# Two mixture-of-experts stages: in-place dot product rows, and semaphores that count diagonals and products by fours

## Chip, cores and metric

The kernel runs on one core of one Trainium2 chip. The metric is the device time of one execution in microseconds, and each time below is the median of three runs.

## What is computed

Two transformer blocks follow each other on 256 tokens of width 1024, all in float32. Each ends in a "PEER" layer, the expert stage, and this is the part that the change touches. Cut to what matters:

```python
q = (xt @ w_pq).reshape(T, 8, 2, 128)              # T = 256 tokens, 8 heads
s = einsum('thpd,hpnd->thpn', q, subkeys)          # scores against 128 keys, twice per head
... top 16 of each, top 16 of their 256 sums ...   # 16 expert numbers per token and head
act = gelu(einsum('thkd,td->thk', peer_u[eb], xb)) * gb      # peer_u, peer_v: 16384 rows of 1024
out = einsum('thk,thkd->td', act, peer_v[eb])
```

For every token and each of its 8 x 16 = 128 experts, one row of `peer_u` is fetched for a dot product with the token, and one row of `peer_v` is fetched and added with the resulting weight. That is 256 x 128 x 2 rows of 4 KB per stage.

## The kernel before, in words

Tokens lie on the 128 partitions, in two tiles T. One "row" i of the stage (`ROWS` = 256, i = 0..255) is one expert slot of one tile: a gather by GpSimd (POOL) brings 128 table rows, one per partition, 512 KB. Rows 0 to 127 are tile 0 and rows 128 to 255 tile 1; sixteen rows in sequence are one head g of a tile. For each row i there is an up gather u(i) (`gather_u`, L2196) and a value gather v(i) (`gather_v`, L2211), 512 gathers per stage. Each engine has its own instruction order and only semaphores tie them together:

- **POOL** issues the gathers in a fixed order: u(0) to u(5), then value and up gathers in turn. Four value gathers are skipped around u(14) to u(21), so from there on the order is ..., v(j), u(j+10), v(j+1), u(j+11), ... An up row may be overwritten eight rows later, when its dot product is done (`u_used`). A value gather waits until the product that last used its slot is done (`pe_used`).
- **VectorE (DVE)** does the dot product of row i (L2038), writing the elementwise product to one of two junk buffers `uj` and the sum to `hidden`. It also does the top-k work of later heads, in parts between dot products, and `weigh(g)`: the weights of head g come right after the dot product of row 16(g+1).
- **ScalarE (ACT)** makes, for each row j, a 128x128 diagonal matrix of the 128 weights (L2162), in a ring of `DIAGS` = 12. It also copies query and score results of later heads out of PSUM (L2078, L2086).
- **TensorE (PE)** multiplies diagonal by value row (L2334) and accumulates in PSUM: two `mm` calls of 512 columns, which the trace shows as four MATMULs. This is called a product below. Before products 8, 20, 36 and 52 it computes a query (L2244, `QUERY_BEFORE`), and right after those products the query's scores (L2257).
- In the last head (rows 240 to 255) six of the rows are added by VectorE (L2061, `LAST_VEC`), so TensorE has 250 products per stage.

The value slots are a ring of `VRING` = 20, but eight of them hold query weights or up rows at first and are released one pair after each query. So the ring is short early in the stage (the code is `free`, `slots`):

```python
free = [(n + RING) % (VRING - RING) for n in range(VRING - RING)]     # 12 slots
slots = list(free)
for p in range(RAW):                                                  # RAW = 4
    slots += free + [VRING - RING + 2 * p, VRING - RING + 2 * p + 1]
```

Value row 12 takes the slot of row 0, row 20 that of row 8, row 34 that of row 20, row 50 that of row 36, row 51 that of row 37; rows 54 to 65 take slots used 14 rows before, and from about row 68 on it is the slot used 20 rows before.

Of the kernel before, what the change touches and what calls it, by code (L numbers as in the profile page):

```python
# [14 lines left out]
P = 128  # L15
S = 256
NT = S // P
# [29 lines left out]
U_AHEAD = 6  # L47
LEAD_GROWS = range(14, 22)
QUERY_BEFORE = {8: 6, 20: 7, 36: 8, 52: 9}
DIAGS = 12  # L50
LAST_IN_RING = 2
LAST_VEC = [2, 5, 7, 10, 13, 15]
SHIFTS = 3
# [1621 lines left out]
def stage_peer(K, rows, sk, nkeys, sk_dma, table_u, table_v, gelu, after, second, queries, out=None, unit=None):  # L1675
# [23 lines left out]
    with ExitStack() as ctx, nc.Block() as block:  # L1699
# [16 lines left out]
        xT = sb("xT", [P, KD, S])  # L1716
        ub = K.wring.rearrange("p a b -> p (a b)").rearrange("p (r d) -> p r d", d=D)
        first_row = 2 * K.query_slot
        uj = sb("uj", [P, D])[:, :], sb("uj", [P, D])[:, :]
        tss, tsd, tiv = (sb(n, [P, NT * after]) for n in ("tss", "tsd", "tiv"))  # L1720
        stored = sg("stored")
        diag = sb("diag", [P, DIAGS, P])
# [89 lines left out]
        def on_tensor(j):  # L1812
            return j if j < FIRST_LAST else FIRST_LAST + sum(1 for i in range(FIRST_LAST, j) if not on_vector(i))

        in_more = [j for j in range(ROWS) if slots[j] < VRING - RING]
        more_tensor, more_vector = ([j for j in in_more if on_vector(j) == which][-1] for which in (False, True))

# [8 lines left out]
        @block.sync  # L1826
        def _(sp):
            for p in queries[1]:
                if p in (2, 3):
                    sp.wait_ge(wlo.sem, PARTS * (second.units[p][0] + 1))  # L1830
                K.load_query(sp, queries[0], p, rows)
            K.reloads = second.units[-1][0] + 1
            K.load_gains(sp)
            sp.wait_ge(normed.sem, normed.at(NT))
            K.gains_used += 1
            K.load_gains(sp)
            if out is not None:
                for T in range(NT):
                    sp.wait_ge(normed.sem, normed.at(NT + T + 1))
                    sp.dma_start(out[T * P:(T + 1) * P, :], K.XN[:, T, :]).then_inc(stored.sem, stored.up(16))  # L1840
                sp.wait_ge(stored.sem, stored.n)
            else:
                sp.wait_ge(u_used.sem, u_used.at(ROWS))
                v_arrived(sp, ROWS - 3)
                K.load_limit = len(K.units)
                for n in range(RAW):
                    if n == RAW - 1:
                        sp.wait_ge(pe_used.sem, pe_used.at(ROWS - len(LAST_VEC)))
                        sp.wait_ge(vec_used.sem, vec_used.at(len(LAST_VEC)))
                    K.load_unit(sp)  # L1850

        @block.vector
        def _(v):
# [134 lines left out]
            def weigh(g):  # L1988

                v.wait_ge(g_exp.sem, g_exp.at(g + 1))  # L1990
                ve.reciprocal(ginv[:, g % 2:g % 2 + 1], gsum[:, g % 2:g % 2 + 1]).then_inc(g_inv.sem, 1)
                if g >= 2:
                    v.wait_ge(dia.sem, dia.at(TOPK * (g - 1)))
                v.wait_ge(g_inv.sem, g_inv.at(g + 1))
                v.wait_ge(act_r.sem, act_r.at(g + 1))
                ve.scalar_tensor_tensor(out=weight[:, g % 2, :], in0=active[:, g % 2, :], scalar=ginv[:, g % 2:g % 2 + 1],
                                        in1=gate[:, g % 2, :], op0=ALU.mult, op1=ALU.mult).then_inc(wts.sem, 1)

            def add_tokens(T):

                v.wait_ge(pe_used.sem, pe_used.at(on_tensor(PER_T * (T + 1))))
                ve.tensor_tensor(K.X[:, T, :], K.X[:, T, :], ps[:, 2 * T:2 * T + 2, :].rearrange("p b c -> p (b c)"),
                                 ALU.add).then_inc(out_r.sem, 1)

# [25 lines left out]
            for g in range(HEADS):  # L2030
                for s in range(TOPK):
                    i = g * TOPK + s
                    u_arrived(v, i)
                    if i >= 2:
                        v.wait_ge(u_used.sem, u_used.at(i - 1))
                    if i % PER_T == 0:
                        v.wait_ge(x_ps.sem, x_ps.at(g // PH + 1))
                    ve.scalar_tensor_tensor(out=uj[i % 2], in0=u_row(i), scalar=1.0, in1=tokens(g // PH),  # L2038
                                            op0=ALU.mult, op1=ALU.mult, accum_out=hidden[:, g % 2, s:s + 1]).then_inc(u_used.sem, 1)
                    if s == 0 and g:  # L2040
                        weigh(g - 1)
                    elif g == PH + 2 and s == TOPK - 2:
                        add_tokens(0)
                    for k in range(after):
                        if g == PH + 4 + 2 * k and s == 10:
                            scaled(v, 0, k)
                    for at, n in ((1, 1), (13, 2), (22, 3)):
                        if 0 <= i - at < TK_PARTS:
                            top_k(n, i - at)
                    if g >= 2 and g + 2 < HEADS and 1 <= s <= TK_PARTS:  # L2050
                        top_k(g + 2, s - 1)
# [19 lines left out]
        def _(act):  # L2071
# [73 lines left out]
            for g in range(HEADS):  # L2145
                act.wait_ge(u_used.sem, u_used.at(TOPK * (g + 1)))
                nc.scalar.activation(active[:, g % 2, :], hidden[:, g % 2, :], gelu).then_inc(act_r.sem, 1)
                act.wait_ge(wts.sem, wts.at(g + 1))
                for s in range(TOPK):
                    j = g * TOPK + s  # L2150
                    if on_vector(j):
                        continue
                    if j - 4 in QUERY_BEFORE:
                        query(QUERY_BEFORE[j - 4])
                        scored(QUERY_BEFORE[j - 4])
                        if QUERY_BEFORE[j - 4] == QSTEPS - 1:
                            act.wait_ge(q_out.sem, q_out.at(QSTEPS))
                            tokens_out(1)
                    n = on_tensor(j)
                    if n >= DIAGS:  # L2160
                        act.wait_ge(pe_used.sem, pe_used.at(n - DIAGS + 1))
                    nc.scalar.activation(diag[:, n % DIAGS, :], K.ident[:, :], ACT.Copy,  # L2162
                                         scale=weight[:, g % 2, s:s + 1]).then_inc(dia.sem, 1)
                for k in range(after):
                    if g == PH + 2 + 2 * k:
                        square(act, 0, k)
                if g + 1 < HEADS:
                    gate_exp(g + 1)
            if unit:
                act.wait_ge(pe_used.sem, pe_used.at(on_tensor(more_tensor) + 1))  # L2170
                act.wait_ge(vec_used.sem, vec_used.at(LAST_VEC.index(more_vector - FIRST_LAST) + 1))
                for half in range(2):
                    act.wait_ge(second.done.sem, second.base + len(second.units) + half + 1)
                    nc.scalar.activation(K.XNT[0][:, half * 4:half * 4 + 4, 0:P],
                                         ps[:, 2 * NT + half, :].rearrange("p (k t) -> p k t", k=4), ACT.Copy).then_inc(t_act.sem, t_act.up())
# [7 lines left out]
        def _(pool):  # L2183
# [15 lines left out]
            def gather_v(j):  # L2199

                n = v_slot(j)
                sig = v_in[n] if n < VRING else u_in[last_ring(n)]
                if n >= VRING:
                    pool.wait_ge(u_used.sem, u_used.at(ROWS))
                elif v_use(j):
                    pool.wait_ge(pe_used.sem, pe_used.at(max(m for m in range(j) if slots[m] == n) + 1))
                elif n >= VRING - RING:
                    home_free(pool, RAW + (n - VRING + RING) // 2)
                elif n < RING:
                    pool.wait_ge(u_used.sem, u_used.at(n + 1))  # L2210
                nc.gpsimd.indirect_dma_start(value_slot(n), None, table_v, bass.IndirectOffsetOnAxis(  # L2211
                    ap=idx[:, j // PER_T, j % PER_T:j % PER_T + 1], axis=0)).then_inc(sig.sem, 16)
# [14 lines left out]
        def _(pe):  # L2227
# [92 lines left out]
            for j in range(ROWS):  # L2320
# [4 lines left out]
                    query(QUERY_BEFORE[j])  # L2325
                if unit and j == FIRST_LAST - TOPK:
                    first_columns()
                pe.wait_ge(dia.sem, dia.at(n + 1))
                v_arrived(pe, j)
                if j == PER_T:  # L2330
                    pe.wait_ge(s_out.sem, s_out.at(QSTEPS))
# [1 line left out]
                for c in range(2):  # L2333
                    last = mm(ps[:, 2 * T + c, :], diag[:, n % DIAGS, :], value_slot(v_slot(j))[:, c * BANK:(c + 1) * BANK],  # L2334
                              start=j % PER_T == 0, stop=ends)
                last.then_inc(pe_used.sem, 1)
                if j in QUERY_BEFORE:
                    score(QUERY_BEFORE[j])
            if unit:
                first_product()  # L2340

        for sig, by in ((tk, TK_EARLY + TK_STEPS * HEADS), (picked, HEADS + 1), (u_used, ROWS), (pe_used, ROWS - len(LAST_VEC)),
                        (vec_used, len(LAST_VEC)), (dia, ROWS - len(LAST_VEC)), (out_r, NT), (x_ps, NT), (g_exp, HEADS), (g_inv, HEADS),
                        (act_r, HEADS), (wts, HEADS), (ready, HEADS),
                        (q_ps, QSTEPS), (q_out, QSTEPS), (s_ps, QSTEPS), (s_out, QSTEPS)):
            sig.up(by)
# [219 lines left out]
```

## Time and profile before

| | us |
|---|---|
| three unprofiled runs, median (lowest, highest) | 1973.23 (1970.73, 1973.85) |
| the profiled execution, first to last instruction | 2142.0 |
| PE busy | 1722.3 |
| DVE busy | 1254.5 |
| POOL busy | 1008.5 |
| ACT busy | 616.9 |

The page gives the profiled execution no other time than its span. It is 168.8 us (8.6%) longer than the unprofiled median, so durations of single instructions and gaps have to be read with care: some gaps of the trace don't exist without the profiler. Times of rows are microseconds from the span's start. In a row of the timeline the first number is the start, the second the duration, and the bracket at the end is the idle time of that engine before it and what ended that.

### The profile page before, as it was taken

The page shows a single profiled execution, that of the slowest core. Times are in us where ns is not written, and L with a number is a line of the kernel's source. Part 1 is how long each engine was busy: PE and PEld are TensorE (multiplying, and loading weights), DVE is VectorE, ACT ScalarE, POOL GpSimd, SP SyncE. Part 2 cuts the span into 40 slices and gives each one's busy share as a digit, 9 for nine tenths or more (in the row PEclk, how much of TensorE's full clock was granted, in tenths as well). Part 3 has the DMA queues.
Part 4 walks back from the last instruction along what each step waited for, and adds up shares of the span by engine and source line. Part 5 has one row for each costly group of instructions (what it writes and reads, how often), then busy time and mean ns, then how long its engine had stood idle before and what let it go on. Part 6 is the DMA issues. An engine that isn't in the chain of part 4 may idle for free. (4 is left out here: it accounts for less than half of the span.)

```text
span 2142.0 us, 22067 instructions
## 1 busy us (share of the span) xinstructions
PE 1722.3 (80%) x7643; PEld 1082.0 (51%) x7643; DVE 1254.5 (59%) x2789; ACT 616.9 (29%) x1151; POOL 1008.5 (47%) x1095
## 2 busy tenths in 40 slices
PE   8999999978787686768668999877777867677768
PEld 7998898844443232323224999754442322222323
DVE  6544665885565665566453456685555566476553
ACT  4472644412121111222213455312212111212212
POOL 3021000366666666667672000265666666666663
PEclk9998999989998787878778999898997878788878
DMA  7521553999999999999997756598999999999996
GB/s 253 165 82 60 172 188 116 307 365 341 347 371 373 351 367 383 352 366 368 361 391 241 232 161 197 187 338 332 342 367 375 361 364 370 365 372 370 359 376 240
DMA packets 243719, 644.22 MB, mean 301 GB/s; under 512 B 19541, under 2 KB 105354, under 8 KB 243610
## 3 DMA queue, kind: packets, MB, share of 16 engines
q0 software_dynamic: 147456, 536.94, 66.3%
q1 hardware_dynamic: 96154, 105.88, 15.4%
q8 instruction: 62, 1.02, 0.2%
q14 instruction: 47, 0.39, 0.0%
HBM read 641.69 MB, written 1.05 MB: 300 GB/s over the span
## 5 line engine op out<-in xcount | busy, mean ns | idle before, releaser
L2038 DVE SCALAR_TENSOR_TENSOR ex_uj<-wring,ps 128x1024 f32<-128x1024 f32 x496 | 601.8, 1219 | 409.7 <-DMA wring<-in_peer_u,ex_idx 363.7
L2334 PE MATMUL ps<-ex_v,ex_diag 128*128 128x512 f32 x1328 | 664.6, 647 | 168.4 <-issue 162.6
L2196 POOL DMA_INDIRECT wring<-in_peer_u,ex_idx x496 | 468.6, 945 | 176.1 <-issue 141.4
L2334 PEld LDWEIGHTS ps<-ex_v,ex_diag 128*128 128x128 f32 x1328 | 270.6, 206 | 546.2 <-issue 535.0
L2334 PE MATMUL ps<-value_rows,ex_diag 128*128 128x512 f32 x664 | 360.0, 677 | 135.4 <-issue 134.0
L2211 POOL DMA_INDIRECT ex_v<-in_peer_v,ex_idx x336 | 318.1, 947 | 242.3 <-remote 110.8
L2162 ACT ACTIVATE ex_diag<-ident,ex_weight 128x128 f32<-128x128 f32 x500 | 171.0, 393 | 720.0 <-remote 390.1
L2334 PEld LDWEIGHTS ps<-value_rows,ex_diag 128*128 128x128 f32 x664 | 141.7, 215 | 351.0 <-issue 345.4
L208 DVE TENSOR_TENSOR w_lo<-wring,w_hi 128x1024 fp32r<-128x1024 f32 (+1 forms) x160 | 187.3, 1211 | 108.4 <-ACT w_hi L199 106.1
L2196 POOL DMA_INDIRECT ex_v<-in_peer_u,ex_idx x16 | 16.4, 1023 | 464.1 <-PE ps L283 459.9
L2211 POOL DMA_INDIRECT value_rows<-in_peer_v,ex_idx x172 | 164.2, 955 | 96.3 <-remote 47.2
L199 ACT ACTIVATE w_hi<-wring 128x1024 fp32r<-128x1024 f32 (+1 forms) x160 | 158.2, 1039 | 80.8 <-PE ps L575 35.3
L575 PE MATMUL ps<-XNT_high,w_hi 128*128 128x256 f32 x328 | 94.1, 287 | 0.5 <-DVE w_lo L208 0.3
L575 PE MATMUL ps<-XNT_low,w_hi 128*128 128x256 f32 x328 | 93.8, 286 | 0.0
L575 PE MATMUL ps<-XNT_high,w_lo 128*128 128x256 f32 x328 | 93.7, 286 | 0.0
L245 PE MATMUL ps<-XNT_high,w_hi 128*128 128x256 f32 x288 | 86.3, 300 | 1.0 <-PEq L510 1.0
L245 PE MATMUL ps<-XNT_low,w_hi 128*128 128x256 f32 x288 | 82.4, 286 | 0.0
L245 PE MATMUL ps<-XNT_high,w_lo 128*128 128x256 f32 x288 | 82.3, 286 | 0.0
L2078 ACT ACTIVATE ex_query<-ps 128x512 f32<-128x512 f32 (+1 forms) x20 | 10.2, 511 | 244.1 <-remote 216.3
L2244 PE MATMUL ps<-ex_xT,wring 128*128 128x128 f32 (+1 forms) x384 | 61.1, 320 | 9.5 <-DVE ex_xT L1985 7.6
L2244 PE MATMUL ps<-ex_xT,value_rows 128*128 128x256 f32 x256 | 58.2, 380 | 11.4 <-issue 11.4
L575 PEld LDWEIGHTS ps<-XNT_high,w_hi 128*128 128x128 f32 x328 | 64.0, 195 | 1.0 <-issue 1.0
(470 smaller groups left out, 2465.0 us busy)
## 6 DMA issues: line engine op xcount, KB each, us to landing
wring<-in_w_in SPq DMA_DIRECT2D x42, 1024.0 KB, 5.4
wring<-in_w_ckv SPq DMA_DIRECT2D x8, 1024.0 KB, 5.3
wring<-in_peer_u,ex_idx POOLq DMA_INDIRECT x496
ex_v<-in_peer_v,ex_idx POOLq DMA_INDIRECT x336
wring<-in_w_mix_out SPq DMA_DIRECT2D x4, 1024.0 KB, 6.6
wring<-in_w_cq SPq DMA_DIRECT2D x4, 1024.0 KB, 5.1
wring<-in_w_co SPq DMA_DIRECT2D x4, 1024.0 KB, 5.2
value_rows<-in_w_pq SPq DMA_DIRECT2D x4, 1024.0 KB, 10.3
```

What stands on the lines that cost most here:

```text
L199: self.nc.scalar.activation(self.part(self.w_hi, m, b), self.raw_part(m, b), ACT.Copy).then_inc(self.named("weights_high").sem, 1)
L208: self.nc.vector.tensor_tensor(self.part(self.w_lo, m, b), self.raw_part(m, b), self.part(self.w_hi, m, b).bitcast(F32), ALU.subtract).the ...
L245: last = mm(ps[:, 6 + u % 2, c * S:(c + 1) * S], w[:, i, c * P:(c + 1) * P], x[:, i, :], start=i == 0 and p == 0, stop=i == KD - 1 and p == 2)
L575: last = nc.tensor.matmul(ps[:, bank_of(j), c * S:(c + 1) * S], w[:, i, off + c * P:off + c * P + P], x[:, i, :], start=start, stop=stop, ...
L2038: ve.scalar_tensor_tensor(out=uj[i % 2], in0=u_row(i), scalar=1.0, in1=tokens(g // PH), op0=ALU.mult, op1=ALU.mult, accum_out=hidden[:, g ...
L2078: nc.scalar.activation(qT[:, k % 2, :, t0 * P:t1 * P], ps[:, query_bank(k), :].rearrange("p (c t) -> p c t", c=2)[:, :, t0 * P:t1 * P], AC ...
L2162: nc.scalar.activation(diag[:, n % DIAGS, :], K.ident[:, :], ACT.Copy, scale=weight[:, g % 2, s:s + 1]).then_inc(dia.sem, 1)
L2196: nc.gpsimd.indirect_dma_start(u_row(i), None, table_u, bass.IndirectOffsetOnAxis(ap=idx[:, g // PH, i % PER_T:i % PER_T + 1], axis=0)).th ...
L2211: nc.gpsimd.indirect_dma_start(value_slot(n), None, table_v, bass.IndirectOffsetOnAxis(ap=idx[:, j // PER_T, j % PER_T:j % PER_T + 1], axi ...
L2244: last = mm(ps[:, query_bank(k), c * S + t0 * P:c * S + t1 * P], w[:, i, c * P:(c + 1) * P], xT[:, i, t0 * P:t1 * P], start=c == 0 and i = ...
L2334: last = mm(ps[:, 2 * T + c, :], diag[:, n % DIAGS, :], value_slot(v_slot(j))[:, c * BANK:(c + 1) * BANK], start=j % PER_T == 0, stop=ends)
```

## The change

Two edits, both in the expert stages.

1. The dot product's elementwise output goes over the up row that it reads (`out=u_row(i)`) and no longer to `uj`, and the wait for the dot product two rows earlier, which protected the junk buffer, is gone.
2. `dia` (diagonals made) and `pe_used` (products done) are increased once for each group of four consecutive TensorE rows (`DIAG_GROUP` = 4; the last group has two), not once for each. Everyone who waits for one of them waits for the group: TensorE before the first product of a group for four diagonals, ScalarE before the first diagonal of a group for the group that used its ring places, POOL before a value gather for the whole group in which the slot's last product lies.

```diff
-DIAGS = 12
+DIAGS, DIAG_GROUP = 12, 4
...
-        uj = sb("uj", [P, D])[:, :], sb("uj", [P, D])[:, :]
...
+        def group(j):
+            return on_tensor(j) // DIAG_GROUP
+
+        def groups(j):
+            return -(-on_tensor(j) // DIAG_GROUP)
+
+        TENSOR_ROWS = ROWS - len(LAST_VEC)
+
+        def ends_group(n):
+            return n % DIAG_GROUP == DIAG_GROUP - 1 or n == TENSOR_ROWS - 1
...
-                    v.wait_ge(dia.sem, dia.at(TOPK * (g - 1)))
+                    v.wait_ge(dia.sem, dia.at(groups(TOPK * (g - 1))))
...
                     u_arrived(v, i)
-                    if i >= 2:
-                        v.wait_ge(u_used.sem, u_used.at(i - 1))
...
-                    ve.scalar_tensor_tensor(out=uj[i % 2], in0=u_row(i), scalar=1.0, in1=tokens(g // PH),
+                    ve.scalar_tensor_tensor(out=u_row(i), in0=u_row(i), scalar=1.0, in1=tokens(g // PH),
...
-                    if n >= DIAGS:
-                        act.wait_ge(pe_used.sem, pe_used.at(n - DIAGS + 1))
-                    nc.scalar.activation(diag[:, n % DIAGS, :], K.ident[:, :], ACT.Copy,
-                                         scale=weight[:, g % 2, s:s + 1]).then_inc(dia.sem, 1)
+                    if n >= DIAGS and n % DIAG_GROUP == 0:
+                        act.wait_ge(pe_used.sem, pe_used.at((n - DIAGS) // DIAG_GROUP + 1))
+                    made = nc.scalar.activation(diag[:, n % DIAGS, :], K.ident[:, :], ACT.Copy,
+                                                scale=weight[:, g % 2, s:s + 1])
+                    if ends_group(n):
+                        made.then_inc(dia.sem, 1)
...
-                    pool.wait_ge(pe_used.sem, pe_used.at(max(m for m in range(j) if slots[m] == n) + 1))
+                    pool.wait_ge(pe_used.sem, pe_used.at(group(max(m for m in range(j) if slots[m] == n)) + 1))
...
-                pe.wait_ge(dia.sem, dia.at(n + 1))
+                if n % DIAG_GROUP == 0:
+                    pe.wait_ge(dia.sem, dia.at(group(j) + 1))
                 v_arrived(pe, j)
...
-                last.then_inc(pe_used.sem, 1)
+                if ends_group(n):
+                    last.then_inc(pe_used.sem, 1)
```

No instruction that computes or moves data is added, removed or moved in an engine's order; waits and increments are all that changes, beside the output address.

## Rows read from the trace of the kernel before

**Rows 1.** The page: its span, and the gathers' queue (packets, MB, share).

```profile
span 2142.0 us, 22067 instructions
q0 software_dynamic: 147456, 536.94, 66.3%
```

**Rows 2.** Timeline, POOL: first gathers of the stages, waiting value gathers, u(48).

```profile
404.93 1.17 POOL L2196 DMA_INDIRECT ex_v<-in_peer_u,ex_idx  x1 [236.95 <-PE ps L283]
...
455.72 0.94 POOL L2211 DMA_INDIRECT ex_v<-in_peer_v,ex_idx  x1 [2.48 <-issue]
...
474.87 0.94 POOL L2196 DMA_INDIRECT wring<-in_peer_u,ex_idx  x1 [0.30 <-issue]
479.26 0.94 POOL L2211 DMA_INDIRECT ex_v<-in_peer_v,ex_idx  x1 [3.44 <-remote]
...
482.76 0.94 POOL L2211 DMA_INDIRECT ex_v<-in_peer_v,ex_idx  x1 [1.22 <-PE ps L2334]
...
514.70 0.94 POOL L2196 DMA_INDIRECT wring<-in_peer_u,ex_idx  x1 [0.30 <-issue]
521.85 0.94 POOL L2211 DMA_INDIRECT ex_v<-in_peer_v,ex_idx  x1 [6.22 <-PE ps L2334]
...
533.61 0.94 POOL L2196 DMA_INDIRECT wring<-in_peer_u,ex_idx  x1 [0.30 <-issue]
...
1368.80 0.94 POOL L2196 DMA_INDIRECT ex_v<-in_peer_u,ex_idx  x1 [222.93 <-PE ps L283]
```

**Rows 3.** Windows of 5 us: length, busy by engine, clock, DMA share, GB/s.

```profile
480.00:485.00 5.00, 5.00 (x18) 2.61 (x18) 3.63 (x11) 4.15 (x9) 3.12 (x4) 1.00 0.76 233
485.00:490.00 5.00, 5.00 (x13) 2.18 (x12) 1.23 (x3) 0.69 (x2) 3.76 (x4) 1.00 0.87 269
515.00:520.00 5.00, 2.22 (x3) 1.07 (x4) 1.11 (x6) 0.17 (x1) 0.64 (x1) 0.55 1.00 400
520.00:525.00 5.00, 5.00 (x16) 2.77 (x16) 4.97 (x14) 2.48 (x8) 1.97 (x3) 0.76 0.31 93
525.00:530.00 5.00, 5.00 (x13) 2.17 (x12) 4.93 (x12) 3.95 (x8) 3.78 (x5) 1.00 0.88 301
535.00:540.00 5.00, 5.00 (x13) 2.18 (x12) 2.43 (x4) 0.21 (x1) 3.78 (x5) 1.00 1.02 415
```

**Rows 4.** Lines by tile: the stages' last TensorE products.

```profile
L2334 PE MATMUL ps<-wring,ex_diag x8: 592/592/593, 1163.9 to 2134.0; 128*128 128x512 f32 x8
```

**Rows 5.** Timeline, ACT: the first diagonals of stage one, and a late one.

```profile
451.21 3.61 ACT L2162 ACTIVATE ex_diag<-ident,ex_weight 128x128 f32<-128x128 f32 x12 [2.13 <-issue]
...
704.53 0.40 ACT L2162 ACTIVATE ex_diag<-ident,ex_weight 128x128 f32<-128x128 f32 x1 [10.10 <-issue]
```

**Rows 6.** Timeline, PE and its weight loads: products, queries, scores.

```profile
451.66 16.89 PE L2334 MATMUL ps<-ex_v,ex_diag 128*128 128x512 f32 x32 [11.49 <-issue]
468.39 7.07 PE L2244 MATMUL ps<-ex_xT,value_rows 128*128 128x256 f32 x32
...
479.61 1.16 PE L2257 MATMUL ps<-sk,ex_query 128*128 128x128 f32 x8 [2.43 <-ACT ex_query L2078]
480.61 9.61 PE L2334 MATMUL ps<-ex_v,ex_diag 128*128 128x512 f32 x22
...
514.59 0.38 PE L2244 MATMUL ps<-ex_xT,value_rows 128*128 128x256 f32 x1 [2.41 <-issue]
517.39 1.01 PE L2334 MATMUL ps<-ex_v,ex_diag 128*128 128x512 f32 x1 [2.42 <-issue]
...
542.16 7.13 PE L2334 MATMUL ps<-ex_v,ex_diag 128*128 128x512 f32 x16 [0.37 <-issue]
...
832.73 0.19 PEld L2334 LDWEIGHTS ps<-value_rows,ex_diag 128*128 128x128 f32 x1 [0.24 <-issue]
```

**Rows 7.** Groups by line: the dot products, and VectorE's last-head additions.

```profile
L2038 DVE SCALAR_TENSOR_TENSOR ex_uj<-wring,ps 128x1024 f32<-128x1024 f32 x496 | 601.8, 1219 | 409.7 <-DMA wring<-in_peer_u,ex_idx 363.7 <-issue 41.7 <-remote 1.8
L2061 DVE SCALAR_TENSOR_TENSOR X<-value_rows,ex_weight,X x3: 1273/1275/1283, 1140.0 to 1158.6; 128x1024 f32<-128x1024 f32 x3
```

More of the change, by code:

```diff
@@ L1847, in _ @@
                     if n == RAW - 1:
-                        sp.wait_ge(pe_used.sem, pe_used.at(ROWS - len(LAST_VEC)))
+                        sp.wait_ge(pe_used.sem, pe_used.at(groups(ROWS)))
                         sp.wait_ge(vec_used.sem, vec_used.at(len(LAST_VEC)))
@@ L1999, in add_tokens @@
             def add_tokens(T):
-                v.wait_ge(pe_used.sem, pe_used.at(on_tensor(PER_T * (T + 1))))
+                v.wait_ge(pe_used.sem, pe_used.at(groups(PER_T * (T + 1))))
                 ve.tensor_tensor(K.X[:, T, :], K.X[:, T, :], ps[:, 2 * T:2 * T + 2, :].rearrange("p b c -> p (b c)"),
@@ L2169, in _ @@
             if unit:
-                act.wait_ge(pe_used.sem, pe_used.at(on_tensor(more_tensor) + 1))
+                act.wait_ge(pe_used.sem, pe_used.at(group(more_tensor) + 1))
                 act.wait_ge(vec_used.sem, vec_used.at(LAST_VEC.index(more_vector - FIRST_LAST) + 1))
@@ L2340, in _ @@
                 first_product()
-        for sig, by in ((tk, TK_EARLY + TK_STEPS * HEADS), (picked, HEADS + 1), (u_used, ROWS), (pe_used, ROWS - len(LAST_VEC)),
-                        (vec_used, len(LAST_VEC)), (dia, ROWS - len(LAST_VEC)), (out_r, NT), (x_ps, NT), (g_exp, HEADS), (g_inv, HEADS),
+        for sig, by in ((tk, TK_EARLY + TK_STEPS * HEADS), (picked, HEADS + 1), (u_used, ROWS), (pe_used, groups(ROWS)),
+                        (vec_used, len(LAST_VEC)), (dia, groups(ROWS)), (out_r, NT), (x_ps, NT), (g_exp, HEADS), (g_inv, HEADS),
                         (act_r, HEADS), (wts, HEADS), (ready, HEADS),
```

## Prediction, made before the changed kernel ran

> **What bounds the kernel now.** I read the page's head first, then windows of the expert stages, then POOL's timeline, in which the row numbers come from counting the gathers along the code's order from the first. The gathers are 536.94 MB of the traffic [rows 1] and run from 404.93 to just after 1163.9 us and from 1368.80 to just after 2134.0 [rows 2, 4]: 761 and 767 us, together 1528 with what follows the last product. All other work is 2142 - 1528 = 614 us, and the change doesn't touch it. Without the profiler the median is 1973.2, so the two stages take about (1973.2 - 614) / 2 = 680 us each. That is the number to explain. One gather is 536.94 MB / 1024 = 0.524 MB. The full rate of a window is 415 GB/s [rows 3], which is 1.263 us a gather and 647 us for 512. POOL issues a gather every 0.94 + 0.30 = 1.24 us when nothing holds it [rows 2], 637 us for 512. The two paces are within 2% of each other, and each fills all but some 35 us of the 680; first arrivals, waits early in the stage and the last products take the rest. So an expert stage is a stream of gathers with no reserve, and whatever holds POOL's queue is paid unless transfers are piled up behind it.
>
> Are they? Look at u at 514.70 followed by v(34) at 521.85 [rows 2]: 7.15 us between issues in place of 1.24, so POOL missed 5.9. The windows there carried 400, 93 and 301 GB/s, against 415 later [rows 3]: that is 0.2 + 3.9 + 1.4 = 5.5 us of lost transfer. At v(20) and v(21) POOL missed 3.1 + 1.0 = 4.1, and the windows at 233 and 269 GB/s lost 2.2 + 1.8 = 4.0. **A wait of POOL is lost nearly one for one**; the pile covers about half a microsecond.
>
> The 169 us by which the profiled execution is longer are stretches in which all engines crawl together: a diagonal after 10.1 us of idleness, matmuls 2.4 us apart [rows 5, 6]. The arithmetic above (680 against 647) leaves no room for them without the profiler, so I take them out wherever they stand in the steps below.
>
> **The change part by part.**
>
> *In-place dot product and its removed wait.* The output row costs nothing or little: 1219 ns now with its output elsewhere; VectorE's other operation of this kind writes over its own input from SBUF at 1275 [rows 7]. The bounds are 0 and +56 ns, 29 us of VectorE over both stages; it lies in the 363.7 us in which VectorE waits for gathers anyway. Without that cover, in the first 30 rows of a stage where VectorE has top-k work, it would be 30 x 0.056 = 1.7 us a stage. The nearest row to the new form is its own old form (one input in PSUM), so I take 0. The removed wait was for a dot product two rows back on the same in-order engine, satisfied whenever it is reached: 0.
>
> *Fewer increments and waits, TensorE and ScalarE.* Per stage 187 waits for `dia` and 187 increments of `pe_used` go. Weight loads of products in one burst are 0.19 + 0.24 = 0.43 us apart, four to a product, 1.72 [rows 6]; loads of a burst stand at this pitch inside a product and from one product to the next, so the wait and the increment cost nothing that a pitch read to 0.01 us shows. I take 0; the other end is 0.02 us a product, 10 us for the 500 of both stages, if TensorE's chain set the end. The Trainium skill speaks otherwise ("TensorE: Matmul & The Clock Gate", section "The cost: per-tile semaphore tail"): increments on completion serialize at some 26 ns each. By that rule 374 fewer would give about 10 us, 1963. No run here shows it, and the row of the weight loads has no such gap.
>
> *Four diagonals before the first product.* Diagonals are 3.61 / 12 = 0.30 apart [rows 5]. Where TensorE waits for a head's first diagonal it now starts 3 x 0.30 = 0.9 us later.
>
> *Slots freed by fours.* This is the term that counts, and it is a new wait. POOL's queue holds up gathers behind a value gather: of both kinds, the up rows for the next head included.
> 1. **v(12)** needs product 0, and was issued at 455.72 after 2.5 us of idleness. It will need product 3. The 32 MATMULs from 451.66 are products 0 to 7, ending at 468.55; 4 x 1.72 before that, 461.67, product 3 ends. With 0.9 for the diagonals and 0.27 to the issue: 462.8, 7.1 later.
> 2. **v(20)** needs product 8, issued at 479.26; it will need product 11. Products 9, 10, 11 run from 480.61, ending at 485.8; +0.9 + 0.27: 487.0, 7.7 later. This doesn't add to the first, since head 0's products don't depend on gathers still to come; the later v(12) is absorbed in it. v(21), which waited for product 9 and was issued at 482.76, follows 2.49 behind at 489.5: from here POOL is **6.7** late.
> 3. **v(34)** needs product 20, which will be 23; its chain starts at u(32), which is now late with POOL, so a delay here adds. Take the same loop one head later for durations: u(48) at 533.61 to product 32 at 542.16 is 8.55; four products 7.13; a query 7.07; the fifth product 1.72; sum 24.5 [rows 2, 6]. POOL gets from u(32) to v(34) in 1.24 + 11 x 2.49 = 28.6. So without the slow stretch (POOL waited 6.22 there only because the query and product 20 crawled) it doesn't wait now, with 3.9 to spare. After: + 0.9, + scores 1.16, + 3 x 1.72 = 7.2, so 31.7 + 0.27 against 28.6: **3.3**.
> 4. **v(50)**: needs product 36, then 39, with query 8 between: the same loop from u(48), another **3.3**.
> 5. Later: v(54) needs product 43, 4 x 1.72 = 6.9 after 39, and comes 10 us later: free. From row 68 the slot is 20 rows old. v(16g+20) comes 33.6 us after u(16g+16), and its group is done 8.55 + 0.9 + 7.1 = 16.6 after it; 17 us to spare. The diagonal ring: diagonal n waits for product n - 9 in place of n - 12, still 8 products (13.8 us) ahead of 1.2 us of work.
>
> Sum per stage: 6.7 + 3.3 + 3.3 = 13.3 us of POOL, of which piled-up transfers cover 0.5 a wait and somewhat more at the first, 2 in all: 11.3 lost. They aren't won back, since transfers at 1.263 are slower than POOL at 1.24. Stage two has the same code with the same first phase. Two stages: +22.6 us. Against the profiled execution that is 2142 + 23 = 2165, there perhaps more, since with slow stretches v(34) and v(50) have no spare; against the median 1973.2 + 22 = **1995 us**, 1.1% slower.
>
> **The rivals.**
> - *Faster: instructions that only wait do cost.* Gone are 254 waits of VectorE and 187 of TensorE a stage, by the code, 882 of the 22067 instructions [rows 1]. If a product has the 0.02 us of its own that the pitch can hide, 10 us come back (500 x 0.02) while the new waits are covered: 1963. For it: the crawl exists, its cause isn't in the rows, and part of the 33 us a stage over the 647 could be of its kind. Against: the even pitch of 0.43, and a TensorE with idle time between heads. The rule of "TensorE: Matmul & The Clock Gate" above would come out at this time too. It decides if the waits of 1, 3 and 4 together lose under 5 us a stage. Chance 0.14.
> - *No change: POOL's new waits are covered.* More transfers are piled up without the profiler than in the windows, or the loops 3 and 4 keep their spare of 3.9 plus a few, and the first wait is won back before row 60. Then 1973, within 4 us. Against: 5.5 of 5.9 us lost at v(34). Chance 0.17.
> - *Only the first wait remains*, 6.7 - 1 a stage, the loops being shorter than I took them: 1985. Part of "slower", 0.20.
> - *Forecast*, all three waits, 1989 to 2002: 0.40.
> - *More than that*: nothing covered (13.3), the last head's products 0.9 later at the end of the stage where value rows and products finish together, the in-place cost of 1.7: 15.9 x 2 = 32, 2005 or above. Chance 0.09.
>
> **How the numbers follow.** The likeliest case gives 1995. Its own range is 1989 to 2002. For 8 in 10 the range has to take in the covered case and leave most of the faster one out: 1968 to 2005. A measurement of this kernel tells 0.2% (4 us) from no change. Faster 0.14, same 0.17, slower 0.69.
>
> **What would show it.** In the changed kernel's timeline v(12) is issued some 7 us later after its up gather than now, and v(13) to v(15) follow without any wait; v(20), v(34) and v(50) wait for PE, longer than v(12)'s present 2.5 us; the 5 us windows behind them fall under 300 GB/s; v(21), v(35), v(51) don't wait. Dot products remain at 1219 ns and products at 1.72. Behind row 68 no value gather waits for PE outside of a slow stretch. I'm wrong if POOL's time from its first gather to v(60) doesn't grow by some 10 us, if the windows stay full through the new waits, or if the products' pitch falls below 1.72, which would make the first rival right.

## The result, and the profile after

The changed kernel is 1.3% slower: 1994.89 us (median of 4, 1992.99 to 1998.98) against 1971.98 for the kernel before (median of 4, 1966.92 to 1973.85). The ratio is 1.0131, 95% interval 1.011 to 1.0151. The forecast was 1995.0. The two medians are 22.9 us apart, 11.5 a stage, against 11.3 in the sum. The ratio isn't exactly the quotient of the medians (that is 1.0116 here) and says 25.8 us, 12.9 a stage. A repetition below, with 22 runs of the kernel before and again four of the changed one, puts the ratio at 1.0139, some 14 us a stage, so the sum was somewhat low. Four single executions among the runs below took 3258 to 7518 us and are left out of every ratio.

First the page of the changed kernel: head, clock and rate over 40 slices of the span, and the dot product's group.

```profile
span 1997.3 us, 21187 instructions
PEclk9989799998899888888889999988999877888779
GB/s 251 178 85 44 118 202 190 162 338 336 369 377 409 409 410 409 409 409 409 409 409 372 253 179 121 225 331 349 367 379 409 409 409 409 409 409 409 410 409 307
L2046 DVE SCALAR_TENSOR_TENSOR wring<-wring,ps 128x1024 f32<-128x1024 f32 x496 | 605.4, 1221 | 429.5 <-DMA wring<-in_peer_u,ex_idx 426.2
```

880 instructions are gone from the program (22067 in [rows 1]), the dot product takes 1221 ns where it took 1219 [rows 7], and once a stage is well under way the gathers stream at a flat 409 GB/s. Within a stage the rate is below that in its first three or four slices (336, 369, 377; then 331, 349, 367, 379) and in its last. The execution timed with this profile took 1998.98 us and its span is 1997.3: nothing separates profiled and unprofiled time here.

Next the timeline of POOL in the changed kernel, the same places as in [rows 2]. In order: u(0), u(21), v(12), v(13), v(20), v(21), u(32), v(34), v(35), v(50), v(51).

```profile
411.34 1.17 POOL L2206 DMA_INDIRECT ex_v<-in_peer_u,ex_idx  x1 [242.39 <-PE ps L283]
...
454.73 0.93 POOL L2206 DMA_INDIRECT wring<-in_peer_u,ex_idx  x1 [0.30 <-issue]
465.33 0.94 POOL L2221 DMA_INDIRECT ex_v<-in_peer_v,ex_idx  x1 [9.67 <-PE ps L2345]
...
467.81 0.94 POOL L2221 DMA_INDIRECT ex_v<-in_peer_v,ex_idx  x1 [0.30 <-issue]
...
486.87 0.93 POOL L2221 DMA_INDIRECT ex_v<-in_peer_v,ex_idx  x1 [1.71 <-PE ps L2345]
...
489.34 0.94 POOL L2221 DMA_INDIRECT ex_v<-in_peer_v,ex_idx  x1 [0.30 <-issue]
...
493.07 0.94 POOL L2206 DMA_INDIRECT wring<-in_peer_u,ex_idx  x1 [0.31 <-issue]
...
526.96 0.93 POOL L2221 DMA_INDIRECT ex_v<-in_peer_v,ex_idx  x1 [4.86 <-PE ps L2345]
...
529.44 0.94 POOL L2221 DMA_INDIRECT ex_v<-in_peer_v,ex_idx  x1 [0.30 <-issue]
...
572.01 0.94 POOL L2221 DMA_INDIRECT ex_v<-in_peer_v,ex_idx  x1 [5.04 <-PE ps L2345]
...
574.49 0.94 POOL L2221 DMA_INDIRECT ex_v<-in_peer_v,ex_idx  x1 [0.30 <-issue]
```

The gap in front of v(12) is 9.67 us, where it was 2.48; v(34) and v(50) wait 4.86 and 5.04. The gathers with a lower number in the same group (v(13), v(35), v(51)) wait for nothing, because one increment frees all four slots. This is what the forecast asked the reader to look for, with one exception: it had v(20) wait longer than 2.5 us, and the wait is 1.71.

What the gaps do to the transfers is in the windows of 5 us (columns as in [rows 3]; the last is GB/s):

```profile
460.00:465.00 5.00, 5.00 (x13) 2.19 (x12) 4.93 (x13) 0.00 (x0) 0.00 (x0) 0.99 0.09 34
465.00:470.00 5.00, 5.00 (x13) 2.18 (x12) 0.07 (x2) 0.00 (x0) 3.74 (x4) 1.00 0.56 174
470.00:475.00 5.00, 5.00 (x20) 3.61 (x19) 2.14 (x8) 0.00 (x0) 3.75 (x4) 1.00 0.91 297
485.00:490.00 5.00, 5.00 (x13) 2.23 (x12) 3.85 (x12) 1.36 (x2) 2.68 (x4) 1.00 1.03 407
525.00:530.00 5.00, 5.00 (x13) 2.13 (x12) 2.03 (x4) 2.59 (x5) 2.43 (x3) 1.00 0.42 129
530.00:535.00 5.00, 5.00 (x13) 2.24 (x12) 1.23 (x2) 0.00 (x0) 3.78 (x5) 1.00 0.94 316
535.00:540.00 5.00, 5.00 (x13) 2.09 (x11) 1.70 (x3) 0.00 (x0) 3.78 (x5) 1.00 0.98 367
```

Against 409, the first three lose 4.6 + 2.9 + 1.4 = 8.8 us for a gap of 9.67, and the last three 3.4 + 1.1 + 0.5 = 5.1 for 4.86. Only v(20) loses nothing (407): its gap of 1.71 is short enough for what is piled up. Here the forecast's sign, a window under 300 behind each wait, didn't come either.

### The profile page after: what moved, and what is told of

Read it like the earlier page. It is cut to its first block and busy times, and to the rows that moved or that the text cites. A ratio compares the mean times of both kernels' runs of the same rounds, so it can differ in the third digit from the quotient of the medians.

```text
span 1997.3 us, 21187 instructions
## 1 busy us (share of the span) xinstructions
PE 1639.4 (82%) x7643; PEld 1072.9 (54%) x7643; DVE 1261.6 (63%) x2789; ACT 600.5 (30%) x1151; POOL 1003.8 (50%) x1095
## 5 line engine op out<-in xcount | busy, mean ns | idle before, releaser
L2046 DVE SCALAR_TENSOR_TENSOR wring<-wring,ps 128x1024 f32<-128x1024 f32 x496 | 605.4, 1221 | 429.5 <-DMA wring<-in_peer_u,ex_idx 426.2
L2345 PE MATMUL ps<-ex_v,ex_diag 128*128 128x512 f32 x1328 | 631.5, 634 | 212.1 <-ACT ex_diag L2170 210.2
L2345 PE MATMUL ps<-value_rows,ex_diag 128*128 128x512 f32 x664 | 312.0, 626 | 95.3 <-ACT ex_diag L2170 94.1
L2345 PEld LDWEIGHTS ps<-value_rows,ex_diag 128*128 128x128 f32 x664 | 132.1, 201 | 268.8 <-issue 163.0
L2170 ACT ACTIVATE ex_diag<-ident,ex_weight 128x128 f32<-128x128 f32 x500 | 152.9, 388 | 239.2 <-PE ps L2345 159.1
L2155 ACT ACTIVATE ex_active<-ex_hidden 128x16 f32<-128x16 f32 x32 | 6.9, 215 | 609.8 <-DVE wring L2046 609.8
L575 PEld LDWEIGHTS ps<-XNT_high,w_lo 128*128 128x128 f32 x328 | 63.7, 194 | 0.0
## 6 DMA issues: line engine op xcount, KB each, us to landing
value_rows<-in_w_pq SPq DMA_DIRECT2D x4, 1024.0 KB, 10.1
```

The costliest lines, as they stand in the source:

```text
L575: last = nc.tensor.matmul(ps[:, bank_of(j), c * S:(c + 1) * S], w[:, i, off + c * P:off + c * P + P], x[:, i, :], start=start, stop=stop, ...
L2046: ve.scalar_tensor_tensor(out=u_row(i), in0=u_row(i), scalar=1.0, in1=tokens(g // PH), op0=ALU.mult, op1=ALU.mult, accum_out=hidden[:, g % ...
L2170: made = nc.scalar.activation(diag[:, n % DIAGS, :], K.ident[:, :], ACT.Copy, scale=weight[:, g % 2, s:s + 1])
```

## The experiments

Each was timed in five rounds against the kernel before on the same chip; every ratio is to that. The first four ran on one chip, on which every kernel, the one before too, takes nearly 9% longer (2140.32 against 1968.21), so a ratio, and no time, is carried from one chip to another. The next four rows of the table ran on a second chip and the last four on a third, both of the usual speed. All but the repetition of the change are built on one variant of it, in which the size of a group is a function of the row number, for each semaphore by itself:

```diff
-DIAGS, DIAG_GROUP = 12, 4
+DIAGS = 12
+DIA_SIZE, PE_SIZE = (lambda n: 4), (lambda n: 4)
```

| | time | before | ratio | 95% |
|---|---|---|---|---|
| in place only | 2138.54 | 2140.32 | 0.9993 | 0.9975 to 1.0011 |
| groups only | 2159.49 | 2140.32 | 1.0083 | 1.006 to 1.0106 |
| diagonals by four | 2139.75 | 2140.32 | 0.9997 | 0.9981 to 1.0014 |
| products by four | 2159.62 | 2140.32 | 1.0082 | 1.0059 to 1.0106 |
| the whole change | 1994.26 | 1968.21 | 1.0139 | 1.0124 to 1.0154 |
| both by two | 1970.74 | 1968.21 | 1.0014 | 1.0002 to 1.0027 |
| two more slots | 1961.64 | 1968.21 | 0.9968 | 0.9956 to 0.998 |
| two more slots, by four | 1969.24 | 1968.21 | 1.0004 | 0.9991 to 1.0017 |
| fours from row 68 | 1967.33 | 1968.41 | 0.9999 | 0.999 to 1.0009 |
| fours until row 68 | 1994.56 | 1968.41 | 1.014 | 1.0124 to 1.0157 |
| in place only, again | 1966.13 | 1968.41 | 0.9992 | 0.9981 to 1.0002 |
| products by four, again | 1987.84 | 1968.41 | 1.0105 | 1.0091 to 1.012 |

### The parts, each alone

**In place only.** The dot product over its up row, its wait gone, both semaphores counted by ones.

```diff
+DIA_SIZE, PE_SIZE = (lambda n: 1), (lambda n: 1)
```

> The dot product over its own up row and without its wait; diagonals and products counted one by one, as before. Slot theory (the loss is value gathers held up because slots come free by fours): no such wait here, so the time of before, 1972, within 4 us. Rival (instructions that only wait cost time): 508 of the 882 are gone, so some 6 us come back, 1966. Rival (the in-place write slows VectorE): 1976 or more, with the dot product's mean above 1221 ns. The profiled execution of before was 2142 and that of the changed kernel 1997.3: if the crawling stretches come with VectorE's extra wait instructions, this one is profiled at about 1975; if they come with the semaphore traffic of ScalarE and TensorE, at about 2140.

**Groups only.** Both by four, dot products into `uj` with their wait, as before.

```diff
-                    ve.scalar_tensor_tensor(out=u_row(i), in0=u_row(i), ...
+                    if i >= 2:
+                        v.wait_ge(u_used.sem, u_used.at(i - 1))
+                    ve.scalar_tensor_tensor(out=uj[i % 2], in0=u_row(i), ...
```

> Junk buffers and their wait kept; diagonals and products counted by fours. Slot theory: all of the loss, 1995 within 4 us. Rival (the in-place write is part of the loss): clearly under 1995. Profiled: the opposite of the run with the in-place row alone, about 2140 if VectorE's waits make the crawl, about 2000 if the one-by-one counting does.

**Diagonals by four**, products by ones.

```diff
+DIA_SIZE, PE_SIZE = (lambda n: 4), (lambda n: 1)
```

> In-place row; diagonals counted by fours, products one by one. Slot theory: slots come free as before, only the first product of a head starts 0.9 us later (three more diagonals); that moves v(12) and v(20) by 0.9 and is within the spare of the later ones: 1 us a stage, 1974. Rival (TensorE's later start is the loss, through heads that follow each other without a gap): 16 heads by 0.9 a stage, 29 us, 2001.

**Products by four**, diagonals by ones.

```diff
+DIA_SIZE, PE_SIZE = (lambda n: 1), (lambda n: 4)
```

> In-place row; products counted by fours, diagonals one by one. Slot theory: the loss without the 0.9 us: v(12) 6.2 late, POOL 5.8 late after v(21), then 2.5 at v(34) and 2.5 at v(50), less 2 covered: 8.8 a stage, 1990. Rival (diagonals by fours are the loss): 1972.

In place only is 0.9993 and, on a chip of the usual speed, 0.9992: no change that can be told. Groups only is 1.0083 and products by four 1.0082: on this chip counting the products by four is the whole loss. Diagonals by four alone are 0.9997.

The traces of the faster chips have no stretches in which all engines crawl, so two of the four were repeated on one, each as it is above:

> The in-place row alone a second time, since its first measurement was on a chip where all kernels took 2140 us. If this chip is like that of the changed kernel (before near 1970): ratio 1.000, as there (0.9993). Rival (without the long stretches the removed waits of VectorE show): 0.997.

> Products by fours, diagonals one by one, a second time for the same reason. Where before takes 1970: slot theory without the 0.9 us, 17.6 us, ratio 1.009; what is missing to the changed kernel's 1.013 is the diagonals' part, v(12) and the loops of v(34) and v(50) each 0.9 later. Rival (the diagonals' 0.9 us is free, as their own run said): 1.013.

**The change itself** once more, with more runs of the kernel before.

> The changed kernel itself once more, beside the others of this group. In the last group of runs the kernel before took 2140 us, 8.5% more than in the first measurement, and all its neighbours with it, so a time is read by its ratio to the kernel before on the same chip. Slot theory: a ratio of 1.009 to 1.013, as products by fours alone gave 1.008 there. If the longer time comes with the chip, the kernel before lies near 1972 or near 2140 and nowhere between.

It is 1.0139, and products by four are 1.0105, on another chip of the same speed. Fours until row 68, below, has diagonals by four too and ran on the same chip as products by four: 1.014. So on these chips the diagonals add some 0.0035 (6.7 us) once products are by four. On the slower chip they added nothing, alone (0.9997) or with the products (1.0083 against 1.0082), and on a faster chip they weren't timed alone. That the 0.9 us go into waits with room when they come alone, and lie in front of waits without room in the change, is argued from the table below and not shown by a run.

### Where in the stage

**Fours from row 68, ones before**, and **fours until row 68, ones after**: the first removes only instructions behind the early waits, the second replaces the early waits only.

```diff
+DIA_SIZE, PE_SIZE = (lambda n: 1 if n < 68 else 4), (lambda n: 1 if n < 68 else 4)
```

> In-place row; rows 0 to 67 counted one by one, from row 68 on by fours (both semaphores). Slot theory: from row 68 the slot is 20 rows old and nothing waits, so nothing is lost: ratio 1.000, although 91 of the 125 or so groups of a whole stage, and with them most of the removed waits, are there. Rival (the later start of each head by 0.9 us, or any cost of fours in the long middle part, is the loss): 12 of 16 heads, 1.010. Rival (fewer semaphore operations are worth something): 0.996.

```diff
+DIA_SIZE, PE_SIZE = (lambda n: 4 if n < 68 else 1), (lambda n: 4 if n < 68 else 1)
```

> The complement: in-place row, rows 0 to 67 counted by fours, all later ones one by one. Slot theory: the whole loss of the changed kernel, ratio 1.012 to 1.014. Rival (loss spread over the stage): a quarter of it, 1.003.

The split is complete: 0.9999 and 1.014. The whole loss is in the first 68 of 256 rows, and the fewer waits and increments of the other 182 products of a stage (272 instructions fewer by the pages of this kernel and of in place only, 21289 against 21561) give nothing that can be told.

POOL's list of waits shows the same (total, times, longest). The four rows, in this order, are of the change, of in place only (again), of both by two and of two more slots:

```profile
POOL ex_v L2221 <- PE ps L2345: 43.0, 22, 9.7
```
```profile
POOL ex_v L2225 <- PE ps L2349: 25.4, 58, 3.1
```
```profile
POOL ex_v L2225 <- PE ps L2349: 22.1, 21, 5.6
```
```profile
POOL ex_v L2227 <- PE ps L2351: 16.2, 53, 0.3
```

With many entries of 0.3 in such a row (the 0.3 that every gather has in front of it), the longest says more than the total.

The table is POOL's position at six places: issue of the value gather minus issue of u(0), mean of both stages, from the timelines. In stage one of the change v(12) is 465.33 - 411.34 = 53.99. For in place only (again), which stands for the kernel before here, u(0), v(12), v(34) and v(50) of stage one are:

```profile
404.25 1.17 POOL L2210 DMA_INDIRECT ex_v<-in_peer_u,ex_idx  x1 [235.44 <-PE ps L285]
...
451.66 0.93 POOL L2225 DMA_INDIRECT ex_v<-in_peer_v,ex_idx  x1 [3.06 <-PE ps L2349]
...
507.90 0.93 POOL L2225 DMA_INDIRECT ex_v<-in_peer_v,ex_idx  x1 [0.30 <-issue]
...
547.66 1.18 POOL L2225 DMA_INDIRECT ex_v<-in_peer_v,ex_idx  x1 [0.30 <-issue]
```

| us after u(0) | v(12) | v(20) | v(34) | v(50) | v(60) | v(255) |
|---|---|---|---|---|---|---|
| in place only | 46.9 | 68.2 | 103.3 | 143.1 | 168.2 | 657.1 |
| the change (profile after), later by | 6.9 | 7.1 | 12.2 | 17.4 | 17.2 | 14.2 |
| fours until 68, later by | 6.6 | 6.8 | 11.9 | 17.1 | 16.9 | 14.3 |
| products by four, later by | 6.7 | 6.9 | 9.8 | 13.9 | 13.7 | 10.9 |
| both by two, later by | 3.0 | 3.1 | 3.9 | 5.0 | 4.9 | 3.0 |
| fours from 68, later by | 0.8 | 0.1 | 0.3 | 0.4 | 0.2 | 0.4 |

Twice the last column is the loss: the change is 1.0139 - 0.9992 = 0.0147 of 1968 us slower than in place only, 28.9 us, or 14.5 a stage against 14.2; products by four 22.2 us, 11.1 a stage against 10.9. For both by two it fits less well: 4.3 us, 2.2 a stage against 3.0, from one trace and an interval of about 0.001 on either side.

### How the loss depends on the slack

**Both by two.**

```diff
+DIA_SIZE, PE_SIZE = (lambda n: 2), (lambda n: 2)
```

> As the changed kernel, with groups of two in place of four. Slot theory: v(12) waits for product 1 and v(20) for product 9, which puts POOL 2.8 us late after v(21); at v(34) and v(50) 24.5 + 0.3 + 1.16 + 1.72 + 0.27 = 28.0 stays under 28.6, so neither waits. 2.3 us a stage, 4.6 in all: ratio 1.0023. Rival (a loss that grows evenly with the group, a third of 23): 7.7 us, ratio 1.004. Rival (the number of semaphore operations counts): faster than before, 0.998.

A third of the group's extra products costs a fifth (3.0 of 14.2): v(20) is 3.1 late, but v(34) and v(50) together add only 1.9. The expectation that these two wouldn't wait at all was wrong: v(34) waits 1.9 us in stage one, v(50) 1.5 in both stages.

**Two more slots.** The junk buffers' 8 KB a partition hold two more value rows. In place, both by ones, and the slots of the last rows put in an order that fits 22:

```diff
-RING, VRING = 8, 20
+RING, VRING = 8, 22
...
+DIA_SIZE, PE_SIZE = (lambda n: 1), (lambda n: 1)
...
-            slots.append(min(range(VRING), key=lambda n: max(j for j, m in enumerate(slots) if m == n)))
+            left = len(slots) - (ROWS - LAST_IN_RING - VRING)
+            among = range(VRING) if left < 0 else range(VRING - RING) if left < VRING - RING else range(VRING - RING, VRING)
+            slots.append(min(among, key=lambda n: max(j for j, m in enumerate(slots) if m == n)))
```

> In-place row, everything counted one by one, and the 8 KB a partition that the junk buffers freed used for two more value slots (22, of them 14 from the start; the last 22 rows take their slots in an order that leaves the stage's end as it is). Row 14, not 12, is the first to take a used slot, row 22 follows row 8. Slot theory: the waits of before at v(12), v(20) and v(21) (2.2 + 3.1 + 0.9 us) go too, POOL is 6 us earlier after row 22 and 5 of them reach the end: 10 us faster in all, ratio 0.995. Rival (POOL's waits early in the stage are covered by piled-up transfers, and the loss of the change has another source): 1.000.

**Two more slots, both by four.** The same with groups of four.

> As the changed kernel, counted by fours, with the two more value slots. Slot theory: v(14) waits for product 3 until 462.8, v(22) for product 11 until 487.0, where the kernel before issued v(22) at 485.25: 1.8 us later; v(36), which now takes the slot of row 20, comes 5 us later in POOL's order than v(34) and doesn't wait. 1.8 us a stage, ratio 1.002. Rival (the loss has to do with fours as such, not with which row waits): 1.011.

With both by one it is 0.9968: 6.3 us faster than the kernel before, where 10 were expected, and the only version here that beats it. Its longest wait for a slot is 0.3 (above). The new order of the last slots wasn't tried without the two slots. With fours and two more slots the ratio is 1.0004: the same coarse count that costs 27 us on a ring of 20 leaves nothing to be told from the kernel before on one of 22, though it still costs 7 us against the same ring by ones; where those lie, no trace here shows. The same run limits another reading of products by four: that edit also makes ScalarE wait for whole groups before it makes diagonals. This wait is the same on the ring of 22, so at most those 7 us can be its doing, and the rest is the wait for slots.

## Why the prediction was right, and where it wasn't

**The stream of gathers with no reserve: right.** So was the step that a wait of POOL is lost nearly one for one: 8.8 of 9.67 and 5.1 of 4.86 us above. Over the 150 us in which all the new waits lie the rate is 360 GB/s in the change (first row) and 402 in the in-place kernel (second), and after it both hold 409:

```profile
451.00:601.00 150.00, 122.43 (x327) 63.71 (x328) 98.02 (x270) 30.46 (x81) 97.37 (x104) 0.89 0.93 360
```
```profile
444.00:594.00 150.00, 135.72 (x385) 73.06 (x386) 109.34 (x299) 36.05 (x93) 110.15 (x117) 0.94 1.02 402
```

150 x (402 - 360) / 409 = 15.4 us. The cover of 2 us was too small, though: of the 17.2 us by which POOL is late at v(60), 3.0 are back at v(255). The full rate is 409 and not the 415 of one window [rows 3]: 1.282 us a gather. So POOL at 1.24 has more room to catch up with the transfers than I took. (512 x 1.24 is 635 us and not 637, which changes nothing else, and the sum itself gives 1973.2 + 22.6 = 1995.8.)

**In place, and instructions that only wait, at nothing: right.** 0.9992 and 0.9993 with 506 instructions fewer (21561 against 22067 in [rows 1]); 0.9999 with 272 waits and as many increments of each semaphore less. The time alone doesn't prove that an increment is free, because behind row 68 the gathers set the pace (409 GB/s in both kernels). TensorE's own pace does: eight products follow each other in the same time in the in-place kernel (first), with an increment at each, and in the change, with one at every fourth.

```profile
617.45 13.90 PE L2349 MATMUL ps<-value_rows,ex_diag 128*128 128x512 f32 x32
```
```profile
639.62 13.90 PE L2345 MATMUL ps<-value_rows,ex_diag 128*128 128x512 f32 x32
```

The Trainium skill ("TensorE: Matmul & The Clock Gate", section "The cost: per-tile semaphore tail") states some 26 ns for each increment, measured on small matmuls that run side by side in the array. By this figure the six increments fewer would have made the second row an estimated 0.16 us shorter, and the trace doesn't agree. The first rival falls with the times and with this row.

The removed waits of VectorE cost nothing that shows either. The Trainium skill ("VectorE: DVE Perf Modes", section "The DRAIN you can't avoid") states that a semaphore after each operation costs nothing extra. The times of in place only agree (0.9992 and 0.9993), but VectorE also idles for gathers for 426.2 us in the profile after, so a small cost wouldn't show in them.

**Step 1 and 2, v(12) and v(20): right in size.** 7.1 was forecast and 6.9 measured for the first, 6.7 and 7.1 for POOL after both, and the second swallows the first as it should (6.9, then 7.1, not 14).

**Steps 3 and 4, v(34) and v(50): the mechanism right, the size wrong.** I took 3.3 each and 5.2 were measured (7.07 to 12.24 and on to 17.39, the table's means with one digit more). The term at fault is the "four products 7.13" of the loop. That row [rows 6] has 0.37 us of idle TensorE in front of it and runs at the full clock. In the changed kernel TensorE has waited longer when a head begins. First the change from product 16 on, then the in-place kernel:

```profile
501.90 10.12 PE L2345 MATMUL ps<-ex_v,ex_diag 128*128 128x512 f32 x16 [8.44 <-ACT ex_diag L2170]
511.86 0.38 PE L2254 MATMUL ps<-ex_xT,value_rows 128*128 128x256 f32 x1
```
```profile
488.70 8.83 PE L2349 MATMUL ps<-ex_v,ex_diag 128*128 128x512 f32 x16 [3.23 <-ACT ex_diag L2174]
497.37 7.07 PE L2258 MATMUL ps<-ex_xT,value_rows 128*128 128x256 f32 x32
```

The four products take 9.96 us from start to the next query's start (511.86 - 501.90) after 8.44 of idleness, and 8.67 after 3.23. The granted clock says why, again the change first (two windows) and then the in-place kernel:

```profile
500.00:505.00 5.00, 3.10 (x4) 1.51 (x5) 3.54 (x13) 2.45 (x8) 3.78 (x5) 0.50 1.03 410
505.00:510.00 5.00, 5.00 (x9) 1.96 (x8) 4.12 (x16) 0.00 (x0) 3.78 (x5) 0.71 1.02 408
```
```profile
488.00:493.00 5.00, 4.29 (x7) 1.83 (x8) 3.61 (x13) 2.45 (x8) 3.78 (x5) 0.69 1.03 409
493.00:498.00 5.00, 5.00 (x14) 2.48 (x13) 4.13 (x13) 0.00 (x0) 3.78 (x5) 0.97 1.03 411
```

0.50 is 1.2 of the 2.4 GHz. The Trainium skill ("TensorE: Matmul & The Clock Gate", section "Part 1: The HAM clock gate") states that the array gets half its clock after an idle time. The trace agrees, with these windows. So the loop feeds on itself: POOL late, weights late, TensorE idle for longer, its first products of the head at the lower clock, the group's last product later, v(34) later.

The length of the idle time alone doesn't fix the duration, though. In stage two of the in-place kernel the same four products take 7.13 us after 1.97 of idleness (the clock is 1.00 there); those of the next head take 9.95 after 6.00, more than the 9.45 after 7.20 in the change:

```profile
1364.24 7.13 PE L2349 MATMUL ps<-ex_v,ex_diag 128*128 128x512 f32 x16 [1.97 <-ACT ex_diag L2174]
1405.78 9.95 PE L2349 MATMUL ps<-ex_v,ex_diag 128*128 128x512 f32 x16 [6.00 <-ACT ex_diag L2174]
```
```profile
547.62 9.45 PE L2345 MATMUL ps<-ex_v,ex_diag 128*128 128x512 f32 x16 [7.20 <-ACT ex_diag L2170]
```

What the two long ones share is the granted clock at their start, 0.50 (the in-place kernel first, then the change):

```profile
1405.00:1410.00 5.00, 4.22 (x5) 1.85 (x6) 3.61 (x13) 2.45 (x8) 3.78 (x5) 0.50 1.03 410
547.00:552.00 5.00, 4.38 (x5) 1.85 (x6) 4.29 (x16) 1.74 (x6) 3.78 (x5) 0.50 1.03 407
```

From u(32) to v(34) it measures 526.96 - 493.07 = 33.9 against my 32.0 (the 24.5 with its additions and the 0.27 to the issue). Of the 1.9 too few, the four products are 2.8 too few; from u(32) to product 16 I had 0.6 too many (8.55 + 0.9 against 501.90 - 493.07 = 8.83), and for the query, the scores and the last four products 0.3 too many. The spare of 3.9 which I gave v(34) holds only where the four products run at the full clock: between the end of the product that it needs and its issue, less the 0.27, there are 4.4 us in stage two of the in-place kernel and 1.5 in stage one (product 20 ends at 506.16, as the trace models it, and v(34) is issued at 507.90). v(50) has 0.2 and 0.0.

The two misses have opposite signs but don't cancel. POOL was 4 us later at v(60) than the sum (17.2 against 13.3), and 1 us more was won back (3.0 against 2), so a stage loses 14.2 and not 11.3. That the forecast of 1995.0 meets the first median of 1994.89 to a tenth is luck: the kernel before measured 1971.98 in those four runs and 1968.2 beside the repetition, where the changed one measured 1994.3.

**Later rows free: right**, by fours from row 68 (0.9999).

**Four diagonals at 0.9: right at the place, wrong as a term of the sum.** From the first diagonal to the first product it is 455.76 - 454.43 = 1.33 us in the change and 447.60 - 447.15 = 0.45 in the in-place kernel. In the table, the change against products by four, that makes 0.2 at v(12) and v(20), where the two stages of one kernel differ by more (53.3 and 53.8 in products by four), then 2.3 at v(34) and 1.0 at v(50), and 3.3 a stage at the end. At v(34) the clock comes on top of the 0.9: products by four has the four products in 500.12 - 491.12 = 9.00 us, the change in 9.96.

**The step that was wrong outright** is the one in which the 169 us of the profile of before were called the profiler's ("leaves no room for them without the profiler, so I take them out"). They belong to the chip, as far as the runs can tell (on which chip the profile of before was taken is not on record). On the chip of the first four experiments 23 timed runs of the kernel before have a median of 2140.32, and the in-place kernel has a span of 2135.9 there and of 1961.5 on another, the same kernel under the same profiler. The crawl that I saw in the rows of before is in TensorE's list of waits (total, times, longest) of its trace. The trace of in place only on the slower chip has such a row too (274.8, 183, 11.6), and those of the change and of in place only on the faster chips have none, so neither the profiler nor the edits make it:

```profile
PE ps L2334 <- issue: 296.6, 208, 11.5
```

The derivation of 680 us a stage survived only because it started from a median of the faster chips (u(0) to the end of the last product is 672 us in the in-place kernel there). On the slower chip the change loses less than on the other (1.0083 against 1.0139, the former with `uj` kept), not more, as the prediction had supposed for stages with slow stretches.

Of the rivals, "no change" fell with the windows at 34 and 129 GB/s, and "only the first wait" with v(34) and v(50). "More than that" had the size of what POOL does but not the time: 2005 would have needed 16 us a stage, and 11.5 to 14.5 were measured, by the medians of the first runs and by the ratio to the in-place kernel.

## What to carry to other kernels

A semaphore that frees ring slots sets how early the next transfer may start; counted by n, every reuse waits for up to n - 1 uses more. Before it is coarsened, find the reuses with the shortest distance in the ring (here those of four gathers among 256 a stage) and compare the extra wait with the spare in front of each. Counting by fours only where the ring is long would have cost nothing, and it gave nothing either; the buffers that the in-place operation set free were worth more as two more slots than both edits together. When a duration of TensorE is taken from another place of the trace for such a sum, look up the granted clock there and ask which clock the new place will have: four products took 7.1 us at the full clock and 8.8 to 10.1 where the clock was 0.5 to 0.7 at their start.

## What the runs showed of the hardware that was not expected

Two chips run one kernel at speeds nearly 9% apart, with no difference in the program. The rate over the 40 slices of the in-place kernel on the slower chip (first) and the faster one:

```profile
GB/s 257 164 80 57 176 188 117 308 361 336 351 375 366 368 374 361 377 360 376 356 377 254 227 148 204 201 320 349 351 368 374 366 362 383 356 374 361 379 375 227
```
```profile
GB/s 252 184 88 45 135 195 188 165 338 387 409 409 409 409 409 409 409 409 409 409 409 357 251 180 111 233 334 394 409 409 409 409 409 409 409 409 410 409 409 294
```

The rate isn't lower throughout: on the slower chip there are windows at the full rate in which TensorE, VectorE and ScalarE do little (2.02, 1.24 and 0.00 us of 5 in the first row below), and then windows that are starved. Two windows of it, two matmuls of the first (or just before it), and the idle time of TensorE's products that no semaphore ended (total, times, longest):

```profile
705.00:710.00 5.00, 2.02 (x2) 0.29 (x1) 1.24 (x4) 0.00 (x0) 2.41 (x3) 0.50 1.02 407
710.00:715.00 5.00, 3.05 (x4) 1.53 (x5) 2.75 (x10) 2.00 (x5) 1.48 (x2) 0.50 0.68 264
```
```profile
703.85 1.01 PE L2349 MATMUL ps<-value_rows,ex_diag 128*128 128x512 f32 x1 [2.91 <-issue]
705.96 1.01 PE L2349 MATMUL ps<-value_rows,ex_diag 128*128 128x512 f32 x1 [1.10 <-issue]
```
```profile
PE ps L2349 <- issue: 274.8, 183, 11.6
```

On the faster chip that last row doesn't exist. The instructions come late on three engines at once while the DMA engines are full. It is neither VectorE's waits nor the counting: all four variants took 2138 to 2160 us there, and the two that were repeated on a faster chip have no such row. Whether instructions are fetched late behind the gathers, or something else holds the engines, stays open; no run here tells.
